# The RWKV stage of a two-block transformer kernel, reordered: gates, key norms, `widen`, mixing and exponentials in new places

## The chip, the cores and the metric

The kernel runs on one core of a Trainium2 chip. The metric is the device time of one execution in microseconds, as the median of several runs. All data is 32-bit floating point.

## What is computed

The reference is a chain of two transformer layers over one sequence of 256 tokens of width 1024. The first layer (two blocks deep, attention and MLP) is not touched. The second mixes tokens by a long convolution (Hyena) and by an RWKV-7 recurrence, weighs both by sigmoid gates, and then runs 16 experts of which each picks its 32 best tokens. What the change touches is this part of the reference:

```python
kk = heads(k * p['rw_k_k']).astype(jnp.float32)
kk = kk * lax.rsqrt(jnp.maximum(jnp.sum(kk * kk, axis=-1, keepdims=True), 1e-24))
k_mod = heads(k * (1.0 + (a - 1.0) * p['rw_k_a']))
...
def step(S, inp):                                   # in each direction, 8 heads of 64
    sa = jnp.einsum('bhij,bhj->bhi', S, a_t)
    S = S * w_t[:, :, None, :] + sa[..., None] * b_t[:, :, None, :] + v_t[..., None] * k_t[:, :, None, :]
    y = jnp.einsum('bhij,bhj->bhi', S, inp[5]) if emit else None
...
y_hy = hyena_branch(hy_cols, p) @ p['hy_proj']
y_rw, finals = rwkv_branch(rw_cols, p, states0)     # head norms, bonus, gate of its own at the end
g_hy, g_rw = jnp.split(jax.nn.sigmoid(gate_cols), 2, axis=-1)
mixed = (g_hy * y_hy + g_rw * (y_rw @ p['rw_proj'])) @ p['w_out']
```

A context of 256 tokens runs through the recurrence in both directions first, and its final states start the recurrence over the 256 tokens of the sequence.

## The kernel before

Weights come from HBM in chunks of 2 MB through SyncE's queue into a ring of four slots, later into more. A chunk is issued when the last job of the chunk that was in its slot is done on TensorE. Each product is a job with a PSUM bank of its own (eight banks in turn). The class `Jobs` writes down the order of jobs, which engine empties each bank, and which job is a chunk's last. `rwkv_steps()` writes down the order of steps in the RWKV stage, and TensorE, VectorE, ScalarE and GpSimd each walk through it and do their part. So the order of steps is the order in all four queues. Every engine works strictly in that order.

**The front.** The raw tiles (`rw` 4 to 11, eight products of 512 columns each over `w_in`) feed the mixing of neighbouring tokens (`mix`, VectorE, six instructions for two tiles) for the context (`ctx`) and the sequence (`lat`). Tiles 8 to 11 are the values. In between stand `lora` (two small products of 64 rows, `lw` and `la`, with sigmoids on ScalarE), `scan` and `centre` (sums of log decays on VectorE), `kraw`, `ksq`, `kk`, `kinv` (the key norm: square on ScalarE, mean over 64 rows on TensorE with a 128 x 128 matrix of 1/64, so that each value appears 64 times, square root on ScalarE, reciprocal and product on VectorE, all over 1024 columns), `exp` (exponentials of the decay sums on ScalarE), `km` and `mul` (the operands, on VectorE). `exp` waits for `kk_ready`.

**The groups.** There are four: g = 0 and 1 are the context forwards and backwards, 2 and 3 the sequence. Each solves a triangular system for its two chunks of 128 tokens: `NT` (scores), masks on GpSimd, `pick`, `spread` and a chain of small VectorE operations (blocks of eight, `blocks_solved`), `widen` (sixteen products with 32 contracted rows each, four for each of four tiles, then a masked copy by VectorE), `T` (transposes), `AK` (scores), then levels 3 to 5 with `W`, `XT` and `T` each, then `W6` and `XT6`. `W` is copied by VectorE; `XT`, `T` by ScalarE. The operands of group n = g + 1 are made inside group g.

**The state chain.** While group g begins, the state of group q = g - 1 is carried over its two chunks: `S0` (scale the state, VectorE), `U0`, `U`, `Y` (only for q of 2 and 3) and `S`, each waiting for the copy of the one before. The loop `for g in range(5)` has a fifth turn with only this chain, for q = 3. Behind it come bonus, group norm of the heads (`gmean`, `gvar`, with a reciprocal of 1024 columns), `gup`, then the eight `gates2` products (L1827), which need the chunks `gates2` 0 to 3, then `branch2`, `wo2`, norms, router and experts. The lines that matter:

```python
out.extend((("hold", 0, k), None, 0, 0, 0, 0, 0) for k in range(4))   # the ring as working space
cols("gates2", "w_in_2", 0, 3328, 5376)
...
elif what == "XT6":                     # releases hold 0, 1; ("S", 3, 1) releases hold 2, 3
    add((what, g, *at), "v", [("hold", 0, 0), ("hold", 0, 1)] if (g, *at) == (3, 1) else [])
```

`gates2` chunk k takes the slot of `hold` k. `product()` and `turn()` (L2529, L2541) are helpers, so most matmuls have one of these two lines. A matmul of 32-bit data appears in the trace as two records.

## Time and profile before

| what | value |
|---|---|
| median of three runs | 2928.76 us (2928.3 to 2930.73) |
| the profiled execution | 2929.43 us, span 2927.6 us |
| TensorE matmul busy | 2596.9 us (89%) |
| VectorE busy | 832.7 us (28%) |
| ScalarE busy | 539.1 us (18%) |
| GpSimd busy | 107.5 us (4%) |
| mean granted TensorE clock | 0.913 |
| from HBM | 663.98 MB, 227 GB/s over the span |

The profile is of one execution; the time of a run holds 1.8 us around the span. A granted clock of 1.00 is 2.4 GHz, 0.50 is 1.2 GHz. Busy shares are averages over stages with different limits, so stages are read by stretches of the timeline: up to some 1315 us the first layer, to 1471 us convolution and raw tiles, to 1841 us the RWKV groups and head norms, to 2052 us gates, output and router, then the experts.

### The profile page before, as it was taken

Reading aid. Unit: us, or ns where it says so; the run is one execution under the profiler, and the core shown is the slowest. Engines: PE = TensorE matmul, PEld = TensorE weight load, DVE = VectorE, ACT = ScalarE, POOL = GpSimd, SP = SyncE. Lnnn points to the kernel's source line nnn. Section 1 sums busy time; section 2 is a strip of 40 time slices with the busy share of each in tenths; the row PEclk is TensorE's granted clock in tenths of the full one; section 3 lists DMA queues with packets and bytes.
Section 4 is the critical chain, followed back from the end, with each engine's and each line's share of the span. In section 5 each row is a group of like instructions: output and inputs, shape, how many; then the busy total and the mean of one; then the engine's idle time right before and its main releaser. Section 6 shows DMA issues by size and latency. Waiting matters only on the chain.

```text
span 2927.6 us, 37135 instructions
## 1 busy us (share of the span) xinstructions
PE 2596.9 (89%) x15696; PEld 1840.4 (63%) x15696; DVE 832.7 (28%) x1479; ACT 539.1 (18%) x1068; POOL 107.5 (4%) x116
## 2 busy tenths in 40 slices
PE   6999999999999999999978899999778677777777
PEld 4757677887757778887568888775334333333333
DVE  2533421002634412002585542222111111111112
ACT  2115411001116211002233422111000000000001
POOL 0100000000100010000011110000000000000000
PEclk8999999999999999999988888998877887888788
DMA  7335755444332663342000001446999999999998
GB/s 303 118 117 226 315 204 201 148 166 182 137 130 87 244 256 134 129 152 103 0 1 1 1 2 58 172 195 254 428 429 429 428 429 427 429 429 428 429 428 359
DMA packets 48721, 666.72 MB, mean 228 GB/s; under 512 B 5498, under 2 KB 5669, under 8 KB 7520
## 3 DMA queue, kind: packets, MB, share of 16 engines
q1 hardware_dynamic: 46656, 656.65, 55.5%
q0 software_dynamic: 1952, 8.40, 0.8%
q8 instruction: 91, 1.49, 0.2%
q14 instruction: 22, 0.18, 0.0%
HBM read 663.98 MB, written 1.05 MB: 227 GB/s over the span
## 4 chain that ended last, share of the span: by engine, by line
PE 67%; DMA 25%; DVE 5%; ACT 2%; issue 1%; POOL 0%; DVEq 0%; POOLq 0%
PE bank L2529 53%; DMA ring<-exp_w 23%; PE bank L2537 7%; PE bank L2541 2%; PE bank L2739 2%; PE bank L1764 1%; DMA arena<-x 1%; PE bank L2558 1%; DMA arena<-exp_w 1%; PE bank L1790 1%; ACT hT L2090 0%; DVE hT L2411 0%; ACT arena L2214 0%; PE bank L2759 0%; DVE arena L1247 0%
## 5 line engine op out<-in xcount | busy, mean ns | idle before, releaser
L2529 PE MATMUL bank<-hT,ring 128*128 128x256 f32 (+2 forms) x3232 | 743.6, 391 | 9.6 <-ACT hT L2090 6.3
L2529 PEld LDWEIGHTS bank<-hT,ring 128*128 128x128 f32 x3232 | 615.0, 195 | 141.0 <-issue 60.8
L2537 PE MATMUL bank<-ring,arena 128*32 128x512 f32 (+1 forms) x2528 | 302.4, 615 | 134.3 <-DMA ring<-exp_w 132.5
L2529 PE MATMUL bank<-arena,ring 128*128 128x256 f32 x1600 | 349.5, 381 | 5.9 <-POOL arena L2062 2.7
L2529 PEld LDWEIGHTS bank<-arena,ring 128*128 128x128 f32 x1600 | 304.6, 191 | 49.0 <-POOL arena L2062 3.6
L2537 PEld LDWEIGHTS bank<-ring,arena 128*32 128x32 f32 x2528 | 83.3, 120 | 300.5 <-issue 191.5
L2537 PE MATMUL bank<-arena 128*32 128x256 f32 (+1 forms) x1552 | 180.2, 626 | 75.6 <-DMA arena<-exp_w 61.6
L2529 PEld LDWEIGHTS bank<-vec,arena 128*128 128x128 f32 x1344 | 181.3, 217 | 85.7 <-issue 78.7
L2529 PE MATMUL bank<-arena 64*128 64x128 f32 (+4 forms) x1156 | 208.1, 377 | 12.2 <-DVE arena L1340 11.3
L2529 PE MATMUL bank<-vec,arena 128*128 128x32 f32 (+2 forms) x1344 | 189.1, 294 | 4.9 <-ACT arena L2095 4.9
L2529 PEld LDWEIGHTS bank<-arena 64*128 64x128 f32 (+1 forms) x1156 | 140.5, 197 | 71.4 <-issue 60.0
L1533 DVE COPY arena<-bank 128x512 f32<-128x512 f32 x64 | 44.3, 692 | 482.6 <-PE bank L2537 482.6
L2537 PEld LDWEIGHTS bank<-arena 128*32 128x32 f32 x1552 | 61.0, 143 | 186.9 <-issue 113.2
L2368 DVE RECIPROCAL arena<-arena 128x512 f32<-128x512 f32 x28 | 93.9, 3353 | 118.4 <-ACT arena L2142 118.4
L2529 PE MATMUL bank<-ring 128*128 128x128 f32 (+1 forms) x1024 | 106.2, 263 | 1.3 <-DVE ring L1350 1.3
L2529 PEld LDWEIGHTS bank<-ring 128*128 128x128 f32 (+1 forms) x1024 | 103.5, 178 | 3.8 <-DVE ring L1350 1.5
L2529 PE MATMUL bank<-ring,hT 128*128 128x512 f32 (+1 forms) x256 | 97.5, 539 | 0.0
L1148 ACT ACTIVATE arena<-bank 128x512 f32<-128x512 f32 x64 | 38.2, 597 | 286.3 <-PE bank L2537 286.3
L2537 PE MATMUL bank<-ring,hT 128*32 128x512 f32 x576 | 70.4, 618 | 14.0 <-DMA ring<-ada_w 14.0
L2529 PEld LDWEIGHTS bank<-ring,hT 128*128 128x128 f32 x256 | 48.6, 190 | 48.4 <-issue 46.9
L1005 ACT ACTIVATE ring<-bank 128x512 f32<-128x512 f32 x112 | 60.9, 603 | 97.9 <-PE bank L2529 57.0
L2492 DVE TENSOR_TENSOR arena<-arena,bank 128x512 f32<-128x512 f32 x32 | 22.0, 688 | 197.7 <-ACT arena L2222 197.7
(306 smaller groups left out, 1974.5 us busy)
## 6 DMA issues: line engine op xcount, KB each, us to landing
ring<-exp_w SPq DMA_DIRECT2D x126, 2048.0 KB, 26.4
arena<-exp_w SPq DMA_DIRECT2D x65, 2048.0 KB, 25.7
ring<-w_in SPq DMA_DIRECT2D x38, 2048.0 KB, 8.2
ring<-ada_w SPq DMA_DIRECT2D x24, 2048.0 KB, 10.0
ring<-w_mlp_up SPq DMA_DIRECT2D x16, 2048.0 KB, 8.3
ring<-w_mlp_down SPq DMA_DIRECT2D x16, 2048.0 KB, 8.1
ring<-mod_w SPq DMA_DIRECT2D x12, 2048.0 KB, 8.3
ring<-w_out SPq DMA_DIRECT2D x6, 2048.0 KB, 8.1
```

The lines of the kernel that those rows point to most:

```text
L1005: free(sc.activation(out_, b, ACT.Identity), key)
L1148: done(sc.activation(raw_row(2 * q), b[:, :], ACT.Identity), ("up1", k0, q))
L1533: done(v.tensor_copy(raw_row(2 * q + 1), b[:, :]), ("up3", k0, q))
L1764: mms.append(nc.tensor.matmul(banks[par][:, p * 64:(p + 1) * 64], a, c, start=(i == 0), stop=(i == 1)))
L1790: mms.append(nc.tensor.matmul(banks[par][part, p * P:(p + 1) * P], a, c, start=(i == 0), stop=(i == 2)))
L2368: chain(v.reciprocal(rs, rs))
L2492: free(v.tensor_tensor(r, r, b[:, :], ALU.mult), ("up", l, i))
L2529: mm = nc.tensor.matmul(out_, a, b, start=(i == 0), stop=(i == len(pairs) - 1))
L2537: mm = nc.tensor.matmul(o, a, b, start=(i < 4), stop=(i >= len(pairs) - 4))
L2541: return nc.tensor.transpose(out_, in_, ident[0:in_.shape[0], 0:in_.shape[0]])
L2558: mm = nc.tensor.matmul(b[:, 0:SEQ], mean1024, sq[:, k], start=(k == 0), stop=(k == KT - 1))
L2739: mm = nc.tensor.matmul(banks[i][:, 0:SEQ], w[:, k, i * P:(i + 1) * P], ar(A_OA, 8, SEQ)[:, k], start=(k == 0), stop=(k == KT - 1))
```

## The change

It reorders the RWKV stage and alters four products in it:

- `gates2` 0 to 3 are steps of the last state chain, 4 stands behind `gmean`, 5 behind `gvar`, 6 and 7 behind `gup`, on TensorE and ScalarE. Their results move from arena column 0 to 10496, and the router's load moves behind the eight additions of `mix`, because it would land there.
- `kk` writes compact norms: four products with 32 output columns each, one below the other in one bank, so that root, `max` and reciprocal run over 256 columns. The new step `kwide` spreads the result over the heads with four products of 32 rows, and VectorE multiplies from the banks. The matrices for both (`C_HEADS`, `C_WIDE`) are loaded behind `solve` over constants that are no longer used.
- `widen` issues its sixteen products across the four row groups in turn, into four banks; `lora` issues `lw` and `la` in pairs.
- In the front, `mix ctx` 8 and 10 go behind `NT` and `widen` of group 0, `rw` 11 behind `mul`; `vt` 0 and `mix lat` 4 go to level 3 of group 0. In group 1, `kinv` goes behind the level-3 `T`, `kwide` ahead of and `exp` behind the level-4 `T`.
- `keep_busy` multiplies a constant into a bank that is written anew afterwards: two pairs of records ahead of `widen` in group 0 and ahead of `U0` of the second chunk, one ahead of its `U` (q below 3).

```diff
@@ rwkv_steps
     yield "rw", 8
+    yield "kk", 0
     yield "rw", 9
-    yield "kk", 0
+    yield "kinv", 0
+    yield "kwide", 0
     yield "rw", 10
-    yield "kinv", 0
     yield "exp", 0
-    yield "rw", 11
-    yield "mix", "ctx", 8
-    yield "mix", "ctx", 10
     yield "km", 0
     yield "mul", 0
-    for g in range(5):
+    yield "rw", 11
+    for g in range(4):
...
             if g == 0:
-                yield "vt", 0
-                yield "mix", "lat", 4
+                yield "mix", "ctx", 8
...
             for tile in range(4):
                 yield "widen", g, tile
+            if g == 0:
+                yield "mix", "ctx", 10
...
                 if lev == 3:
+                    yield "vt", 0
+                    yield "mix", "lat", 4
                     yield "mix", "lat", 6
                     yield "mix", "lat", 8
...
                     yield "vt", 1
-                    yield "kinv", 1
-                    yield "exp", n
...
+            if lev == 4 and n == 2:
+                yield "kwide", 1
             for tile in range(4):
                 yield "T", g, lev, tile
             if lev == 3 and n == 2:
                 yield "kk", 1
+                yield "kinv", 1
+            if lev == 4 and n == 2:
+                yield "exp", n
...
+    yield "S0", 3, 0
+    yield "BK", 3, 0
+    yield "U0", 3, 0
+    yield "BK", 3, 1
+    yield "U", 3, 0
+    yield "Y", 3, 0
+    yield "S", 3, 0
+    yield "S0", 3, 1
+    yield "gates2", 0
+    yield "U0", 3, 1
+    yield "gates2", 1
+    yield "U", 3, 1
+    yield "gates2", 2
+    yield "Y", 3, 1
+    yield "S", 3, 1
+    yield "gates2", 3
@@ Jobs
+    def gates2(self, i):
+        self.add(("gates2", i), "s", [("gates2", 0, i // 2)] if i % 2 else [])
@@ GpSimd
-            pool.dma_start(cst[:, C_SPREAD:], t["solve"]).then_inc(solve_loaded, 16)
+            pool.dma_start(cst[:, C_SPREAD:], t["solve"][:, 0:NCONST - C_SPREAD]).then_inc(solve_loaded, 16)
+            for at, n in ((C_HEADS, 0), (C_WIDE, 1)):
+                pool.dma_start(const(at), t["solve"][:, NCONST - C_SPREAD + P * n:NCONST - C_SPREAD + P * n + P]).then_inc(solve_loaded, 16)
...
-            pool.wait_ge(yrw_ready, 2)
-            pool.dma_start(ar(E_ROUTER, KT, N_EXP), t["router"].rearrange("(a p) n -> p a n", p=P)).then_inc(router_loaded, 16)
-            pool.dma_start(ar(E_SLOTS, CAP), t["slots"]).then_inc(router_loaded, 16)
             for j in range(8):
                 ...
+            pool.dma_start(ar(E_ROUTER, KT, N_EXP), t["router"].rearrange("(a p) n -> p a n", p=P)).then_inc(router_loaded, 16)
+            pool.dma_start(ar(E_SLOTS, CAP), t["slots"]).then_inc(router_loaded, 16)
@@ ScalarE
-                    for hf in range(2):
-                        b = filled(act, ("kk", g, hf))
-                        free(sc.activation(ar(R_ROOT + 512 * hf, 512), b[:, :], ACT.Sqrt, scale=64.0), ("kk", g, hf))
+                    b = filled(act, ("kk", g))
+                    free(sc.activation(ar(R_ROOT, SEQ), b[:, 0:SEQ], ACT.Sqrt), ("kk", g))
@@ VectorE
-                    emptied(dve, ("kk", g, 1))
-                    inv = ar(R_ROOT, 1024)
+                    emptied(dve, ("kk", g))
+                    inv = ar(R_ROOT, SEQ)
                     chain(v.tensor_scalar(inv, inv, 1e-12, None, ALU.max))
-                    chain(v.reciprocal(inv, inv))
-                    v.tensor_tensor(ar(R_KK, 1024), ar(R_KK, 1024), inv, ALU.mult).then_inc(kk_ready, 1)
-                    dve.wait_ge(kk_ready, g + 1)
+                    v.reciprocal(inv, inv).then_inc(kk_inverted, 1)
+                elif what == "kwide":
+                    for ct in range(CT):
+                        b = filled(dve, (what, g, ct))
+                        free(v.tensor_tensor(kk[:, ct], kk[:, ct], b[:, 0:SEQ], ALU.mult), (what, g, ct))
+                    emptied(dve, (what, g, CT - 1))
+                    dve.sem_inc(kk_ready, 1)
@@ TensorE
+                    for ct in range(CT):
+                        mm = product(b[32 * ct:32 * ct + 32, 0:SEQ], [(const(C_HEADS, 32), ar(R_SQ + SEQ * ct, SEQ))])
+                    finish(mm)
+                elif what == "kwide":
+                    pe.wait_ge(kk_inverted, g + 1)
+                    banks = [start((what, g, ct), ct) for ct in range(CT)]
+                    for ct in range(CT):
+                        part = slice(32 * ct, 32 * ct + 32)
+                        finish(product(banks[ct][:, 0:SEQ], [(cst[part, C_WIDE:C_WIDE + P], ar(R_ROOT, SEQ, parts=part))]))
...
+                    banks = [start((what, g, tile), tile) for tile in range(4)]
+                    if g == 0:
+                        keep_busy(banks[0], 2)
                     pe.wait_ge(blocks_solved, g + 1)
                     for p in range(CT):
-                        mm = product(b[:, p * P:(p + 1) * P], [(cst[part, C_WIDEN + P * p:C_WIDEN + P * (p + 1)], solved[part])])
-                    finish(mm)
+                        mms = []
+                        for tile in range(4):
+                            part = slice(32 * tile, 32 * tile + 32)
+                            mms.append(product(banks[tile][:, p * P:(p + 1) * P],
+                                               [(cst[part, C_WIDEN + P * p:C_WIDEN + P * (p + 1)], solved[part])]))
+                    for mm in mms:
+                        finish(mm)
...
+                    if g < 3 and at[0] == 1:
+                        keep_busy(banks[0], 2)          # U0
...
+                    if g < 3 and at[0] == 1:
+                        keep_busy(b, 1)                 # U
...
+            gates(4)                                    # behind gmean
...
+            gates(5)                                    # behind gvar
...
+            gates(6)                                    # behind gup
+            gates(7)
```

## Rows read from the trace of the kernel before

**Rows 1.** The page: GB/s in 40 slices; a DMA issue, KB, us to landing.

```profile
GB/s 303 118 117 226 315 204 201 148 166 182 137 130 87 244 256 134 129 152 103 0 1 1 1 2 58 172 195 254 428 429 429 428 429 427 429 429 428 429 428 359
...
ring<-w_in SPq DMA_DIRECT2D x38, 2048.0 KB, 8.2
```

**Rows 2.** SyncE's timeline of DMA issues: start us, us, what.

```profile
1794.37 35.43 SPq L2027 DMA_DIRECT2D ring<-w_in  x4
...
1924.38 0.80 SPq L2027 DMA_DIRECT2D arena<-exp_w  x2
```

**Rows 3.** Stretches: us, busy time of each engine, TensorE's clock, DMA share, GB/s.

```profile
1471.40:1808.00 336.60, 298.21 (x2812) 276.32 (x2812) 185.24 (x328) 115.60 (x220) 40.81 (x32) 0.86 0.04 14
1808.00:1841.30 33.30, 24.50 (x150) 17.57 (x149) 9.14 (x17) 6.67 (x9) 0.00 (x0) 0.74 0.32 126
```

**Rows 4.** TensorE's timeline, front and prices: start, us, line, op, [idle before <-releaser].

```profile
1425.27 2.96 PE L2529 MATMUL bank<-arena 64*128 64x256 f32 x16
1428.16 27.73 PE L2529 MATMUL bank<-hT,ring 128*128 128x512 f32 x64
...
1482.21 3.78 PE L2529 MATMUL bank<-arena 64*128 64x128 f32 x32 [10.86 <-DVE arena L1340]
...
1499.62 4.97 PE L2529 MATMUL bank<-rope,cst 32*128 32x128 f32 x32 [4.96 <-DVE rope L1368]
...
1671.44 2.06 PE L2529 MATMUL bank<-arena 64*128 64x128 f32 x32
...
1967.78 2.74 PE L1840 MATMUL bank<-cst 128*128 128x512 f32 x6
...
2041.74 1.93 PE L2537 MATMUL bank<-ring,arena 128*32 128x256 f32 x32
```

**Rows 5.** VectorE's timeline, front and prices.

```profile
1472.80 1.80 DVE L1247 SCALAR_TENSOR_TENSOR arena<-arena,vec 128x256 f32<-128x256 f32 x4
1474.76 1.38 DVE L1324 TENSOR_SCALAR arena<-arena,vec,stat 128x256 f32<-128x256 f32 x4 [0.16 <-DVE arena L1247]
...
1480.85 1.22 DVE L1340 SCALAR_TENSOR_TENSOR arena<-arena 128x1024 f32<-128x1024 f32 x1
...
1840.50 6.55 DVE L1425 RECIPROCAL arena<-arena 128x1024 f32<-128x1024 f32 x1 [4.00 <-ACT arena L1115]
...
1958.90 1.75 DVE L1457 RECIPROCAL arena<-arena 128x256 f32<-128x256 f32 x1 [0.93 <-ACT arena L1126]
```

**Rows 6.** TensorE's timeline, groups 1 and 2.

```profile
1563.02 0.63 PE L1764 MATMUL bank<-arena,ring 128*128 128x64 f32 x4 [1.93 <-DVE hT L1389]
...
1569.36 3.65 PE L2529 MATMUL bank<-hT,ring 128*128 128x64 f32 x16 [0.83 <-ACT hT L1005]
1572.94 5.13 PE L2529 MATMUL bank<-rope,cst 32*128 32x128 f32 x32
...
1589.77 3.81 PE L2529 MATMUL bank<-ring 128*128 128x128 f32 x32 [1.30 <-DVE ring L1350]
...
1614.83 3.65 PE L2541 MATMUL bank<-cst,ring 128*128 128x128 f32 x16 [9.76 <-ACT ring L1005]
...
1632.30 4.72 PE L2529 MATMUL bank<-arena 64*128 64x128 f32 x48 [0.47 <-DVE arena L1340]
```

**Rows 7.** Stretches of 2 us: us, TensorE busy, granted clock, DMA share, GB/s.

```profile
1552.00:1554.00 2.00, 2.00 (x11) 0.50 0.00 0
...
1576.00:1578.00 2.00, 2.00 (x15) 0.50 0.00 0
```

**Rows 8.** The chain of waits: start us, us, what (`U0` at either clock).

```profile
1563.02 5.55 PE bank L1764 x32
...
1795.75 3.87 PE bank L1764 x32
```

**Rows 9.** TensorE's timeline, the gates.

```profile
1841.31 55.42 PE L2529 MATMUL bank<-hT,ring 128*128 128x256 f32 x256
```

**Rows 10.** The DMA view: a GpSimd load, KB, us to landing.

```profile
arena<-x POOLq DMA_DIRECT2D x1, 1024.0 KB, 26.2
```

More of the change, by code:

```diff
@@ L81 @@
 NCONST = C_MASKB + 2 * 768
+C_HEADS, C_WIDE = C_MEAN128, C_ROT
 def shape_constants():
@@ L330, in rwkv_steps @@
             yield "S", q, 1
-        if not new:
-            return
         for tile in range(4):
@@ L518, in second_block @@
             elif what == "kk":
+                add(("kk", g), "s")
+            elif what == "kwide":
+                for ct in range(CT):
+                    add(("kwide", g, ct), "v")
+            elif what == "lora":
                 for hf in range(2):
-                    add(("kk", g, hf), "s")
-            elif what == "lora":
-                for half in ("lw", "la"):
-                    for hf in range(2):
+                    for half in ("lw", "la"):
                         add((half, g, hf), "s")
@@ L535, in second_block @@
                 self.raw(g)
+            elif what == "gates2":
+                self.gates2(g)
             elif what == "W" or what == "S":
@@ L544, in second_block @@
                 add((what, g, *at), "v")
-        for what, e in (("bonus", "v"), ("gmean", "v"), ("gvar", "s"), ("gup", "v")):
+        for what, e, *gates in (("bonus", "v"), ("gmean", "v", 4), ("gvar", "s", 5), ("gup", "v", 6, 7)):
             for hf in range(2):
                 add((what, hf), e)
-        for i in range(8):
-            add(("gates2", i), "s", [("gates2", 0, i // 2)] if i % 2 else [])
+            for i in gates:
+                self.gates2(i)
         for j in range(8):
@@ L1037, in second_scalar, with gates @@
             raw(3)
+            def gates(i):
+                b = filled(act, ("gates2", i))
+                free(sc.activation(ar(E_GATES + 512 * i, 512), b[:, :], ACT.Sigmoid), ("gates2", i))
             act.wait_ge(lora_mixed, 1)
@@ L1044, in second_scalar @@
                     raw(g)
+                elif what == "gates2":
+                    gates(g)
                 elif what == "ksq":
@@ L1115, in second_scalar @@
                 free(sc.activation(ar(R_ROOT + 512 * hf, 512), b[:, :], ACT.Sqrt, bias=col("rw_eps")), ("gvar", hf))
-            act.wait_ge(yrw_ready, 2)
-            for i in range(8):
-                b = filled(act, ("gates2", i))
-                free(sc.activation(ar(E_GATES + 512 * i, 512), b[:, :], ACT.Sigmoid), ("gates2", i))
+            for i in range(5, 8):
+                gates(i)
             sc.activation(stat[:, 62:63], eps, ACT.Sqrt)
@@ L1288, in second_vector @@
             for what, g, *at in rwkv_steps():
-                if what in ("rw", "mix"):
+                if what in ("rw", "mix", "gates2"):
                     s, d = None, None
                 else:
-                    s, d = group(2 * g) if what in ("kraw", "kinv") else group(g)
+                    s, d = group(2 * g) if what in ("kraw", "kinv", "kwide") else group(g)
                 if what == "kraw":
@@ L1629, in second_tensor, with keep_busy @@
                                              for m in range(4)]))
+            def keep_busy(b, n):
+                for _ in range(n):
+                    nc.tensor.matmul(b[:, :], ident, cst[:, 0:512], start=True, stop=True)
             pe.wait_ge(lora_loaded, 48)
@@ L1636, in paired, with gates @@
                 return [start((name, g, ci, par), par) for par in range(2)]
+            def gates(i):
+                w = chunk(("gates2", 0, i // 2))
+                columns(("gates2", i), w, (2 * (i % 2), 2 * (i % 2) + 1), lambda k: hT[:, 0, k], KT)
             for what, g, *at in rwkv_steps():
@@ L1640, in second_tensor @@
                     raw(g)
+                    continue
+                if what == "gates2":
+                    gates(g)
                     continue
@@ L1824, in second_tensor @@
                 finish(mm)
-            for i in range(8):
-                w = chunk(("gates2", 0, i // 2))
-                columns(("gates2", i), w, (2 * (i % 2), 2 * (i % 2) + 1), lambda k: hT[:, 0, k], KT)
+            gates(6)
+            gates(7)
             wh, wr = chunk(("hyp", 0, 0)), chunk(("rwp", 0, 0))
@@ L1835, in second_tensor @@
             work = ar(E_WORK, KT, SEQ)
-            def keep_busy(b, n):
-                for _ in range(n):
-                    nc.tensor.matmul(b[:, :], ident, cst[:, 0:512], start=True, stop=True)
             def mean_of(b, ready, i):
```

44 lines of the change are left out of this document (23 added, 21 removed).

## The prediction

> **What bounds the kernel now.** I read the page first. Its GB/s line shows two regimes [rows 1]: from about 2050 us to the end the DMA engines move some 428 GB/s, all they ever do, and between 1460 and 1790 us they move nothing worth naming. So the expert stage is bound by its weights, and the RWKV stage before it by something else. The question for any saving is then whether the expert weights start earlier with it. SyncE's timeline [rows 2] says yes: the first two expert chunks are issued at 1924.38, when the eighth `branch2` product is done, and the next ones at later steps of TensorE. Nothing in that queue starts by a time of its own. A microsecond that TensorE saves before 1924 us moves the whole stream, and I count it in full.
>
> Then I cut TensorE's busy time and clock into stretches [rows 3]. From the last raw tile to the last chain it is busy 298.2 of 336.6 us at a mean clock of 0.86; in the last chain and head norms (1808 to 1841.3) 24.5 of 33.3 us at 0.74. Both idle time and the half clock are there to win. TensorE's timeline and the chain of waits name the places, part by part.
>
> **1. The front: raw tiles, key norm, first operands.** TensorE idles 10.86 us ahead of the first `NT` at 1482.21, released by VectorE's last multiply [rows 4]. VectorE's queue shows why [rows 5]: a reciprocal of 1024 columns (6.55 us, as the one at 1840.50), a product, the mixing of `ctx` 8, then tile 11's copy, the mixing of `ctx` 10 (to 1474.6), then `km` and `mul`, 7.3 us (1474.76 to 1482.07). Now the reciprocal is over 256 columns (1.75 us, as the one at 1958.90) and both mixings come after `NT`. New order by rows: the paired `lora` (part 3) brings all 1.05 us forward. `kk` becomes 8 matmul records with 32 output columns; in [rows 4] 32 such records of 256 columns take 1.93 us, so 0.5 for 8. `kwide` I take at 0.8: bounds 0.5 (four at once) and 8 x 0.217 = 1.7. Raw 8, `kk`, raw 9, `kwide`, raw 10 then end at 1440.95 + 6.93 + 0.5 + 6.93 + 0.8 + 6.93 = 1463.0 (a raw tile is a quarter of the 27.73 us in [rows 4]; tile 7 ended at 1442.0). ScalarE copies tile 10 (0.7), loads its table (1.28) and makes two exponentials (2.1): 1467.2. `km` and `mul` add 7.3 and the issue 0.15: `NT` at 1474.8 against 1482.2. **Gain 7.4.** Raw 11 (to 1469.9) is hidden in this. 5 us of idle time stay.
>
> **2. The first group pays for it.** What was taken off the front isn't gone: `ctx` 8 takes the place of `lat` 4 behind `NT`, so `NT` to solved blocks stays 17.4 us; `ctx` 10 (2.5 us, of which 1.80 are the four instructions in [rows 5]) goes ahead of `scan`, and `lat` 4 joins `lat` 6 and 8 in level 3. Count from the start of `widen` (1499.62). VectorE before: `widen` copies to 5.6, scan and centre to 11.6, `AK` and `W` copies, so `XT` of level 3 at 15.0. Now: `widen` w, four copies 2.5, mixing 2.5, scan 3.4, centre 2.6, `AK` 2.4, first `W` 0.65, issue 0.2: w + 14.3 = 15.8 with w = 1.5. Three mixings (7.45) behind `W` put its level-4 copy at 25.5 and `XT` there at 25.6, not 24.0; the group ends at 40.0 instead of 38.3. **Loss 1.7** (3.2 at half clock). `vt`, 1.1 us of TensorE, lies in the time that TensorE now waits.
>
> **3. `widen` round the row groups, and fillers.** `widen` is 32 records, 4.97 to 5.13 us [rows 4, 6], all at half clock (0.50, [rows 7]). Pairs of 64 rows cost 2.06 us for 32 records at full and 3.78 at half clock [rows 4, 6]. I take w = 1.5 at full (bounds 0.9, four at once at the 0.114 us of a record with 128 rows, and 2.1, no better than pairs) and 3.0 at half. The Trainium skill (TensorEngine Tiling (Array Packing), Theoretical Speedup) allows up to 4 times for 32 rows: by it w is about 1.25, by the pairs 2.1. The same page (Key Properties) says that a change of the tiling mode drains the engine; no row here isolates such a drain.
> `lora` was 2.96 us for 16 records; as pairs I take 1.9 (bounds 1.5 and 2.96): 1.05 each, in groups 0 (counted), 1 and 2.
> What `widen` gives is cut by VectorE. In group 1, before, `widen` start to `XT` of level 3 is 16.8 us, and behind the first copy it is all VectorE: four copies, scan, `S`, centre, `kraw`, `AK`, `W` [rows 6]. Now w + 13.6: 15.1 (gain 1.7) or at half clock 16.6 (0.2). Group 2, without `kraw`: w + 12.5 against 17.4, gain 3.4 or 1.9. Group 3, no scan, TensorE bound: 5.1 - w = 3.6 or 2.1, and `Y` there 1.4 faster at full clock.
> Fillers: two matmul pairs ahead of `U0`, one ahead of `U`. A filler of 512 columns costs 0.91 us (2.74 for three, [rows 4]). They fill waits of 1.93, 1.92 and 1.23 us, and 0.83 us: so they cost 0.1 in groups 1 and 2 and 0.7 in group 3. If they hold the clock, `U0` goes from 5.55 to 3.87 and `U` from 3.65 to about half, 1.94 [rows 6, 8]: 3.4 in groups 1 and 2, and 2.0 in group 3, whose `U0` was slow only at its end. Sums, full or half clock: group 1 1.05 - 0.1 + 3.4 + 1.7 = 6.0 or 1.1; group 2 7.7 or 2.8; group 3 6.3 or 1.4. Does the clock hold? For: a `U0` with next to no idle time ahead (1795.75) runs at full speed. Against: at 1552 us the clock is 0.50 without idle time [rows 7]. I take the middle: 3.5 + 5.2 + 3.9 = **gain 12.6**.
>
> **4. The third exponentials.** In group 1 TensorE idles 9.76 us ahead of the level-4 `T` at 1614.83 [rows 6]. ScalarE stands in its queue at `exp`, which waits for VectorE's `max`, reciprocal (6.55) and product, 8.5 us, and the four `XT` copies stand behind it. Now: `kk` 0.5, table and root to 2.4 behind it, 256-column reciprocal; the first `W` copy of level 4 at 10.7 us after the level-3 `XT` start, so `XT` at 10.8 (one more 0.35 wait), `kwide` to 15.2, `T` to 17.0. `exp` then runs (4.6) under `W` of level 5 (3.7), and `T` ends at 26.2 instead of 38.0. With `W6` and `XT6` 30.2; but `km` and `mul` (9.0) start only when `exp` is done at 22.2, so the next `NT` is at 31.4, not 42.5 [rows 6]. **Gain 11.1**, and a wait of about 1.2 stays ahead of that `NT`.
>
> **5. Gates in the last chain and in the head norms.** All 55.3 us of `gates2` stand behind the norms [rows 9]. From the end of `S` 3,0 (1808.0) to the first `branch2` (1896.56) are 88.6 us. Moved between the links they cover the 8.8 us of idle time and the half clock that [rows 3] show there. At full rate: gates 55.3, `U0` 3.87, `U` 1.94, `Y` 3.9, `S` 1.1, bonus and means 3.7, variances 1.9, `gup` 1.8: 73.5. **Gain 15.1.** Checked: chunk 0 and 1 are issued from 1794.37 [rows 2]; the first lands 8.2 us later [rows 1], at 1802.6, the second one transfer (2 MB at 428 GB/s, 4.9 us) behind it: ahead of the first gate at 1808 and the third at 1819. Chunk 2 can load only once `S` 3,1 is done; the fourth gate (6.9) and bonus and means (3.7) leave it 10.6 us, where such a chunk lands in 8.2 [rows 1]. The tail of norms on VectorE, 12.1 us from its reciprocal (1840.50, [rows 5]) to the last product, starts 0.8 us after the variances; gates 5 to 7 and `gup` (22.5) cover it. ScalarE's extra table loads (1.28 each) lie there too.
>
> **6. The rest, at nothing.** Two more small constant loads stand in GpSimd's queue, which idles 3 us behind the old one. The router's load goes behind the additions of `mix`, into the expert stream; TensorE needs it 42 us later (from about 1926, just behind the first expert chunks in [rows 2], to the fillers at 1967.78 in [rows 4]), and the slowest landing of any GpSimd load is 26.2 us [rows 10].
>
> **Sum.** 7.4 - 1.7 + 12.6 + 11.1 + 15.1 = 44.5 us off the profiled execution's 2929.43: 2884.9; the median of the runs is 0.67 lower: **2884.3 us**. Everything at full clock gives 51.6 (2877), everything in part 3 at half clock 35.5 (2893).
>
> **Rivals.**
> *The clock falls as before* (15%): low-density groups are enough, fillers or not. Gain 32 to 37: 2892 to 2897. For it speaks 1552 us. The Trainium skill (TensorE: Matmul & The Clock Gate, A second HAM failure mode) tells of micro-idles between matmul groups that make the clock oscillate; by that rule this is the outcome.
> *The clock holds everywhere* (17%): 2872 to 2879; it would also lift the 1714 to 1725 stretch, which I left slow.
> *Interleaving gives no overlap* (8%): w = 5.1 and copies that begin only behind it. VectorE's chain starts later than before: 1.9 lost in group 1, like amounts elsewhere; with the full 7.4, 11.1 and 15.1 the gain is 22 to 30: 2899 to 2907.
> *The expert stream hides it* (2%): if the stream had its own start, no change, 2928. Against it: each issue in [rows 2] stands at a TensorE step.
> *Slower* (3%): the router's 1024 small pieces starve beside the expert chunks. Landing 85 us after issue or later (42 of slack plus the 44 saved) decides it; at 100 us it gives 2944. No row is near.
> Forecast, gain 38 to 50: 55%, 2879 to 2891.
>
> The range from 2872 to 2902 leaves out most of the last three and the far half of the no-overlap case. A difference of 0.2% (6 us) is about what this kernel's times can tell from none: faster 0.94, same 0.02, slower 0.04.
>
> **What would show it.** First `NT` near 1475; no wait of 9.8 us ahead of `T`; `widen` under 2 us a group with a clock of 1.00 in `U0` and `U`; no idle time over 1 us from 1800 to the first `branch2`; a stream of expert chunks that starts 44 us earlier. Wrong it would be by a new wait on a chunk of gates, by `W` copies stuck behind the mixings for longer than 2 us, or by a clock of 0.50 where I put 1.00.

## The result

The changed kernel takes 2879.23 us (median of three runs, 2879.03 to 2882.24) against 2928.76 (2928.3 to 2930.73): a ratio of 0.9833, 95% interval 0.9814 to 0.9852. The forecast was 2884.3, its range 2872 to 2902. 49.5 us are gained where 44.5 were forecast. The profiled execution took 2879.03 us with a span of 2876.5; its mean granted clock is 0.930 (0.913 before).

### The profile page after: what moved, and what is told of

It is laid out like the page before. It is cut to its first block, busy times and chain, and to the rows that moved or that the text cites. A ratio compares the mean times of both kernels' runs of the same rounds, so it can differ in the third digit from the quotient of the medians.

```text
span 2876.5 us, 37230 instructions
## 1 busy us (share of the span) xinstructions
PE 2563.0 (89%) x15742; PEld 1806.9 (63%) x15742; DVE 820.3 (29%) x1485; ACT 536.7 (19%) x1066; POOL 108.5 (4%) x118
## 4 chain that ended last, share of the span: by engine, by line
PE 66%; DMA 26%; DVE 5%; ACT 2%; issue 1%; POOL 0%; DVEq 0%; ACTq 0%; POOLq 0%
PE bank L2595 53%; DMA ring<-exp_w 25%; PE bank L2603 7%; PE bank L2607 2%; PE bank L2805 2%; PE bank L1832 1%; DMA arena<-x 1%; PE bank L2624 1%; PE bank L1860 1%; ACT hT L2156 0%; DVE hT L2477 0%; ACT arena L2280 0%; PE bank L2825 0%; DVE arena L1283 0%; DVE ring L1387 0%
## 5 line engine op out<-in xcount | busy, mean ns | idle before, releaser
L2595 PEld LDWEIGHTS bank<-hT,ring 128*128 128x128 f32 x3232 | 607.8, 192 | 139.2 <-issue 63.3
L1216 ACT ACTIVATE arena<-bank 128x128 f32<-128x128 f32 x64 | 17.7, 277 | 320.6 <-PE bank L2595 320.6
```

Of the source, the lines that this page charges most:

```text
L1216: sc.activation(ar(E_SL + 128 * q, 128), b[:, 0:128], ACT.Silu).then_inc(silu_ready, 1)
L2595: mm = nc.tensor.matmul(out_, a, b, start=(i == 0), stop=(i == len(pairs) - 1))
```

## The profile after

The page, GB/s in 40 slices, as in [rows 1]:

```profile
GB/s 310 119 107 230 305 236 205 147 146 205 117 124 111 191 256 173 143 146 114 30 1 2 1 2 59 176 235 314 428 428 429 429 428 429 428 429 428 429 428 356
```

SyncE's timeline, the chunks of gates and the first expert chunks, as in [rows 2]:

```profile
1757.22 45.76 SPq L2093 DMA_DIRECT2D ring<-w_in  x4
...
1871.41 0.80 SPq L2093 DMA_DIRECT2D arena<-exp_w  x2
```

The expert stream still runs at 428 GB/s and starts 53.0 us earlier (1924.38 before; 3.1 of it were there ahead of the first `lora`, where nothing was changed). So what the RWKV stage saved came through to the end, as the forecast had argued from the issue times.

Stretches of the changed kernel: front (first `lora` to first `NT`), groups 0, 1 and 2 (`NT` to the next `NT`), group 3 (to `U0` 3,0), last chain with norms and gates (to the first `branch2`). Columns as in [rows 3].

```profile
1422.20:1471.90 49.70, 44.98 (x129) 19.92 (x129) 22.45 (x43) 15.03 (x30) 0.00 (x0) 0.98 0.00 0
1471.90:1532.90 61.00, 52.91 (x490) 48.96 (x490) 52.13 (x98) 25.22 (x48) 10.59 (x8) 0.91 0.01 1
1532.90:1606.30 73.40, 68.97 (x688) 61.63 (x686) 42.42 (x82) 33.82 (x62) 10.07 (x8) 0.95 0.01 2
1606.30:1680.30 74.00, 71.83 (x726) 65.54 (x726) 44.52 (x83) 30.14 (x57) 10.14 (x8) 0.93 0.01 2
1680.30:1758.60 78.30, 76.10 (x813) 67.88 (x813) 33.45 (x64) 22.24 (x45) 10.07 (x8) 0.96 0.02 4
1758.60:1843.60 85.00, 84.22 (x541) 70.52 (x542) 20.95 (x26) 14.48 (x23) 0.00 (x0) 1.00 0.42 171
```

The same six stretches of the kernel before are 56.9, 59.7, 90.4, 76.6, 86.9 and 100.8 us long, at clocks of 0.94, 0.88, 0.83, 0.89, 0.86 and 0.92. TensorE's busy time fell from 424.1 to 399.0 us and its idle time from 47.2 to 22.4: of the 49.9 us saved, half is idle time. But 10.9 us of the busy time after are the new fillers (22 records of L1674), which do no work of the kernel. Without them TensorE works 388.1 us. So the 49.9 us are 24.8 of idle time and 36.0 of work done faster, less 10.9 for the fillers. TensorE ran at half clock for 109 us between 1300 and 1900 us before, and for 38 now. Read the last row across: in the sixth stretch TensorE is busy 84.22 of 85.00 us at 1.00.

TensorE's timeline, front, against [rows 4]:

```profile
1444.90 0.64 PE L2595 MATMUL bank<-arena,cst 128*32 128x256 f32 x8
...
1452.54 0.71 PE L2595 MATMUL bank<-arena,cst 32*128 32x256 f32 x8
...
1471.91 5.99 PE L2595 MATMUL bank<-arena 64*128 64x128 f32 x48 [4.73 <-DVE arena L1380]
...
1483.37 1.88 PE L1674 MATMUL bank<-cst 128*128 128x512 f32 x4
1489.22 1.24 PE L2595 MATMUL bank<-rope,cst 32*128 32x128 f32 x32 [3.96 <-DVE rope L1408]
```

`kk` and `kwide` take 0.6 to 0.7 us each, the wait ahead of `NT` has shrunk from 10.86 to 4.73, and `widen` takes 1.24 instead of 4.97.

VectorE in the front, against [rows 5]:

```profile
1447.72 1.75 DVE L1342 RECIPROCAL arena<-arena 128x256 f32<-128x256 f32 x1
...
1464.46 1.38 DVE L1364 TENSOR_SCALAR arena<-arena,vec,stat 128x256 f32<-128x256 f32 x4 [9.78 <-ACT stat L1121]
```

VectorE now waits 9.78 us for ScalarE's exponentials ahead of `km`; before, it had waited 0.16 there.

TensorE's timeline, group 1, against [rows 6]:

```profile
1553.40 0.63 PE L1832 MATMUL bank<-arena,ring 128*128 128x64 f32 x4 [0.20 <-DVE hT L1429]
...
1557.19 1.12 PE L1674 MATMUL bank<-cst 128*128 128x512 f32 x2
1558.16 1.91 PE L2595 MATMUL bank<-hT,ring 128*128 128x64 f32 x16
1560.00 1.17 PE L2595 MATMUL bank<-rope,cst 32*128 32x128 f32 x32
...
1567.50 1.16 PE L2595 MATMUL bank<-arena 64*128 64x128 f32 x16 [1.97 <-DVE hT L1445]
1568.59 5.47 PE L2595 MATMUL bank<-ring 128*128 128x128 f32 x32
1574.65 3.81 PE L2595 MATMUL bank<-ring 128*128 128x128 f32 x32 [0.59 <-DVE ring L1390]
...
1589.93 1.97 PE L2607 MATMUL bank<-cst,ring 128*128 128x128 f32 x16
...
1606.28 4.09 PE L2595 MATMUL bank<-arena 64*128 64x128 f32 x36 [1.45 <-DVE arena L1380]
```

Read it from the top. Fillers (L1674) stand where the waits of 1.93 and 0.83 us were, `U` takes 1.91 instead of 3.65, `widen` 1.17 instead of 5.13, `T` of level 4 (1589.93) has no wait of 9.76 us any more, and 1.45 are left ahead of the next `NT`. One line is new: 1.97 us of idle time inside `AK`, released by VectorE's emptying of the bank that `S` had filled (L1445), and behind it `W` at half clock, 5.47 where 3.84 is its full-clock time. The forecast had no such wait.

TensorE's timeline, the first three gates, against [rows 9]:

```profile
1770.80 7.17 PE L2595 MATMUL bank<-hT,ring 128*128 128x256 f32 x32
...
1781.53 15.87 PE L2595 MATMUL bank<-hT,ring 128*128 128x256 f32 x80
```

They fill the state chain (the 15.87 us are two gates and `U`) without a wait between them. No gate waits for its chunk: all of TensorE's idle time in the 85 us is 0.78 us, ahead of the first `Y`.

## The experiments

All times are medians of four or five runs. The kernel before took 2928.2 to 2929.7 us beside them.

**The changed kernel again.** It is told first, since it says how the others are to be read.

> The changed kernel once more, unaltered, to see how far the same code scatters from run to run. If the stretch from the first lora to the first branch2 (421.4 us in its first profile) repeats within 1 us, differences of 5 us between my one-part kernels are theirs. If it moves by 3 to 5 us, with stretches of half clock in other places, then differences of that size in single stretches (the tails of two experiments, 3 to 6 us longer at half clock) belong to the clock and not to the step that was moved.

Measured: 2877.99 us (2876.97 to 2889.51, five runs), ratio 0.9831 (0.9818 to 0.9844). The profiled run was the slowest, and its stretch from `lora` to `branch2` took 433.0 us instead of 421.4, with the same instructions. Its stretches of group 1 and of the last chain (73.4 and 85.0 above):

```profile
1535.80:1614.80 79.00, 73.28 (x688) 65.17 (x686) 42.45 (x82) 33.68 (x62) 10.08 (x8) 0.89 0.01 1
...
1768.70:1857.80 89.10, 88.32 (x540) 73.79 (x541) 20.96 (x26) 14.62 (x23) 0.00 (x0) 0.94 0.40 163
```

The clock is lower in both, 0.89 for 0.95 and 0.94 for 1.00. The stage came only 2.6 us later. Half clock takes 65 us of this profile and 38 of the first. In group 1 it covers `U` and `widen`, though the fillers stand ahead of them:

```profile
1564.11 3.52 PE L2595 MATMUL bank<-hT,ring 128*128 128x64 f32 x16
1567.55 2.09 PE L2595 MATMUL bank<-rope,cst 32*128 32x128 f32 x32
```

So stretches of half clock move from execution to execution and made a difference of 11.6 us in the stage here; the kernel before scatters by 3.7 us in nine runs beside it. A difference of 4 or 5 us in a single stretch is therefore only a part's own where the clock there is the same or where a wait shows it. Pooled, the changed kernel's eight runs have a median of 2879.1 us; I compare with that.

**Gates behind `gup` again.**

```diff
-    yield "gates2", 0        # and 1, 2, 3, between the links
...
-            gates(4)         # gmean
...
-            gates(5)         # gvar
...
+            for i in range(8):
+                gates(i)     # behind gup
```

> The changed kernel with all eight gate products behind the last product of the head norms again. If they cover waits and the half clock there (my theory), it is 15 us slower than the changed kernel (2879.2), so about 2894, and the stretch from the end of the third-last state product to the first product of the two branches takes about 88 us again, not 73. If the gain of the tail came only from idle time and the clock would rise anyway, 9 us: 2888. If the expert stream had hidden it, no difference.

Measured: 2896.11 us (2893.4 to 2903.17), ratio 0.9896 (0.9879 to 0.9912), 17.0 more than the changed kernel. `U0` 3,0 to `branch2` took 100.85 us instead of 84.99. TensorE's timeline shows the old waits:

```profile
1795.80 3.67 PE L2588 MATMUL bank<-arena,cst 128*128 128x512 f32 x8 [3.15 <-DVE arena L1446]
...
1801.49 1.95 PE L2588 MATMUL bank<-arena,cst 128*128 128x512 f32 x4 [2.02 <-ACT arena L1145]
...
1805.01 55.42 PE L2588 MATMUL bank<-hT,ring 128*128 128x256 f32 x256
```

15.9 us for this part: theory held. In this profile, too, the half clock is back for 17 us (1774 to 1791), as before the change.

**No fillers.**

```diff
-                    if g == 0:
-                        keep_busy(banks[0], 2)
...
-                    if g < 3 and at[0] == 1:
-                        keep_busy(banks[0], 2)
...
-                    if g < 3 and at[0] == 1:
-                        keep_busy(b, 1)
```

> The changed kernel without its three new places of filler matmuls; everything else stays. If they hold TensorE's clock in the state chain and at widen (theory), the clock falls to 0.50 in U0, U and widen of groups 1 to 3 and the kernel is 9 to 12 us slower (2888 to 2891), with widen at 2 to 3 us a group instead of 1.2. If the clock would hold without them, because widen and the pairs are short now, it is as fast as the changed kernel or up to 1 us faster.

Measured: 2894.54 us (2893.04 to 2897.36), ratio 0.9881 (0.9865 to 0.9898), 15.4 more. TensorE's timeline of its group 1, `U0`, `U` and `widen`:

```profile
1556.43 0.78 PE L1828 MATMUL bank<-arena,ring 128*128 128x64 f32 x4 [1.93 <-DVE hT L1429]
...
1563.67 3.64 PE L2589 MATMUL bank<-hT,ring 128*128 128x64 f32 x16 [0.83 <-ACT hT L1037]
1567.24 2.09 PE L2589 MATMUL bank<-rope,cst 32*128 32x128 f32 x32
```

The waits of before are back to the hundredth (1.93, 0.83). `U` takes 3.64 and `widen` 2.09, at half clock, here in all three groups; the second profile of the changed kernel has about the same in groups 1 and 2 (3.52 and 2.09) with fillers, and the full clock in group 3 alone. So these rows do not show by themselves what the fillers do. In the profiled executions TensorE ran at half clock for 85 us between 1300 and 1900 us, against 38 in the changed kernel's first profile and 65 in its second. Stretch for stretch against the second, which began at the same time, it lost 6.0 us, against the first 17.6. The median says 15.4, more than the 9 to 12 expected, and the slowest of the changed kernel's eight runs (2889.51) is faster than the fastest here (2893.04). So the fillers earn time, some 15 us by the medians; how much of it in one execution depends on where the half clock falls. They cost little: from the product ahead of them to `U0` TensorE takes 1.92 us in group 1 as before, and in group 3 1.55 for 1.23.

**`widen` one tile after the other.**

```diff
+                    tile = at[0]
+                    part = slice(32 * tile, 32 * tile + 32)
+                    b = start((what, g, tile))
                     for p in range(CT):
-                        for tile in range(4):
-                            mms.append(product(banks[tile][...], [(cst[part, ...], solved[part])]))
+                        mm = product(b[...], [(cst[part, ...], solved[part])])
+                    finish(mm)
```

> The changed kernel with the sixteen products of widen tile by tile again. Theory: the row groups overlap only when they alternate, so widen takes at full clock 2.5 to 3.7 us instead of 1.2, and as VectorE's first copy starts behind a quarter of it, each group loses 0.5 to 2 us: 2 to 6 us in all, 2881 to 2885. Rival: the gain at widen was the clock alone, then widen takes about 2.5 us and nothing is lost that VectorE does not hide: below 1.5 us.

Measured: 2888.68 us (2882.31 to 2895.08), ratio 0.9866 (0.9846 to 0.9886), 9.6 more. TensorE's timeline, `widen` of groups 0 and 1:

```profile
1492.23 5.13 PE L2590 MATMUL bank<-rope,cst 32*128 32x128 f32 x32 [4.31 <-DVE rope L1408]
...
1565.16 2.82 PE L2590 MATMUL bank<-rope,cst 32*128 32x128 f32 x32
```

This splits the term. In the old order the sixteen products cost 2.82 us at full clock (groups 1 to 3) and 5.13 at half; in the new order 1.17. Of the 3.7 to 4.0 us by which the change made `widen` shorter in groups 0 and 1, some 1.65 are the row groups and 2.2 to 2.3 the clock. 2 to 6 us were expected for the whole kernel: a miss in size. The stage was 5.5 us longer than in the first profile of the changed kernel and 6.1 shorter than in the second, and the runs scatter by 12.8 us, so no more than the rows of `widen` themselves can be taken from this run.

**Third exponentials back ahead of the level-4 `T`.**

```diff
                 if lev == 4:
                     yield "vt", 1
+                    yield "kinv", 1
+                    yield "kwide", 1
+                    yield "exp", n
...
-            if lev == 4 and n == 2:
-                yield "exp", n
```

(`kinv` and `kwide` are taken out of their new places too.)

> The changed kernel with kinv, kwide and the third exponentials ahead of the level-4 XT again, the norms still compact. If the order made the gain (theory), TensorE idles again at that place: kwide waits 3 us for the reciprocal and T some 5 us for ScalarE, 7 to 9 us slower than the changed kernel, 2886 to 2888. If the short reciprocal alone made it, under 3 us slower.

Measured: 2883.14 us (2879.47 to 2888.97), ratio 0.9851 (0.9834 to 0.9867), 4.0 more. TensorE's timeline, `kwide` and the level-4 `T`:

```profile
1587.89 0.71 PE L2593 MATMUL bank<-arena,cst 32*128 32x256 f32 x8 [1.90 <-DVE arena L1340]
...
1595.12 2.09 PE L2605 MATMUL bank<-cst,ring 128*128 128x128 f32 x16 [2.75 <-ACT ring L1035]
```

Two waits, 4.65 us, stand where before one of 9.76 stood; `widen` to `W6` of group 1 is 4.8 longer and 1.0 comes back as the wait ahead of `NT`. 7 to 9 were expected, and under 3 by the other theory: a miss in size, between the two. The place alone is worth 3.8 us once the norms are compact.

**Norms over 1024 columns, in the new places.**

```diff
-                    for ct in range(CT):
-                        mm = product(b[32 * ct:32 * ct + 32, 0:SEQ], [(const(C_HEADS, 32), ...)])
-                    finish(mm)
+                    for hf in range(2):
+                        b = start(("kk", g, hf))
+                        finish(product(b[:, :], [(mean64, ar(R_SQ + 512 * hf, 512))]))
```

> The changed kernel with the key norms over 1024 columns again (two products with the mean matrix, a reciprocal of 6.55 us), in the new places. Theory: in the front nothing changes by more than 0.5 us, because the reciprocal ends at about 1459, ahead of the copy of tile 10 that ScalarE waits for; in group 1 the level-4 copies of W wait for it and TensorE idles 6 to 8 us: 2886 to 2888. Rival: the compact norms also set the first NT, then it is 3 us or more later too and the kernel is over 2889.

Measured: 2886.07 us (2882.51 to 2887.74), ratio 0.9848 (0.9833 to 0.9863), 6.9 more. `lora` to `NT` took 49.91 us, `widen` to `W6` of group 1 49.14 instead of 40.81. VectorE's timeline there:

```profile
1586.17 6.55 DVE L1338 RECIPROCAL arena<-arena 128x1024 f32<-128x1024 f32 x1
```

and TensorE's, the level-4 `XT`:

```profile
1594.86 5.59 PE L2580 MATMUL bank<-ring 128*128 128x128 f32 x32 [6.52 <-DVE ring L1382]
```

The expectation was right in time. Compact norms earn 8.3 us from `widen` to `W6` in group 1, because there the reciprocal stands ahead of the `W` copies: 6.5 are this wait and 1.8 the half clock on `XT` behind it (5.59 for 3.81). They earn 0.2 in the front, where VectorE waits for ScalarE anyway.

**The front's old order.**

```diff
     yield "exp", 0
+    yield "rw", 11
+    yield "mix", "ctx", 8
+    yield "mix", "ctx", 10
     yield "km", 0
     yield "mul", 0
-    yield "rw", 11
```

(`vt` 0 and `lat` 4 go back too.)

> The changed kernel with raw tile 11 and both context mixings ahead of km and mul, and vt and the mixing of lat 4 behind NT, as in the kernel before; the norms stay compact. Theory: the first NT is 5 to 6 us later, group 0 gives 1.4 us back, so 4 us slower, 2883. Rival: the compact norms made the gain in the front, then this is within 1 us of the changed kernel.

Measured: 2883.6 us (2878.32 to 2885.57), ratio 0.9838 (0.9823 to 0.9853), 4.5 more. TensorE's timeline, first `NT`:

```profile
1481.60 2.72 PE L2594 MATMUL bank<-arena 64*128 64x128 f32 x22 [10.86 <-DVE arena L1379]
```

10.86 us, the wait of [rows 4] to the hundredth, although the norms are compact here. `lora` to `NT` is 6.1 us longer, `widen` to `W6` of group 0 3.1 shorter: 3.1 net, where 4 were expected. Elsewhere in this profile the last chain is 5.7 us longer at a clock of 0.92, which this edit does not touch and of which the changed kernel's second profile shows 4.2 as well, and groups 1 and 3 are 3.1 shorter.

**`scan` behind `S`,** to remove the new wait inside `AK`.

```diff
-            if ahead:
+            if ahead and g == 0:
                 yield "scan", n
         if old:
...
             yield "S", q, 1
+        if ahead and g > 0:
+            yield "scan", n
```

> The changed kernel with VectorE's scan behind the copies of S in groups 1 and 2. The wait of 1.97 us in the middle of AK goes (AK's last bank is that of S, which VectorE empties behind scan). Theory: group 2 gains 2.4 us, its wait and the half clock of its W (5.46 instead of 3.8 us); group 1 gains nothing at XT, as VectorE's queue ends at the same time; in all 2 to 3 us, 2876 to 2877. Rival: both groups stay bound by VectorE, no difference.

Measured: 2887.72 us (2884.25 to 2890.15), ratio 0.9859 (0.9843 to 0.9874), 8.6 more: a miss, on the wrong side. TensorE's timeline, `AK`, `W` and `XT` of group 1:

```profile
1564.71 2.06 PE L2597 MATMUL bank<-arena 64*128 64x128 f32 x32
1566.70 3.84 PE L2597 MATMUL bank<-ring 128*128 128x128 f32 x32
1574.99 5.93 PE L2597 MATMUL bank<-ring 128*128 128x128 f32 x32 [4.45 <-DVE ring L1392]
```

`AK` has no wait, `W` is at full clock; but VectorE's sum is what it was, so all of it stands as one wait of 4.45 us ahead of `XT`, which starts 14.66 us behind `widen` for 14.65 in the changed kernel and then runs at half clock. That half clock is the 2.1 us by which `widen` to `W6` is longer. In group 2 it is 1.0 shorter, where 2.4 were expected. How much of the 8.6 belongs to that and how much to where the half clock fell is open: see the next pair.

**A front of its own, and with `scan` behind `S`.** The front's mixings go into the time in which VectorE waits there.

```diff
     yield "kk", 0
+    yield "mix", "lat", 4
     yield "rw", 9
     yield "kinv", 0
     yield "kwide", 0
+    yield "exp", 0
+    yield "mix", "ctx", 8
     yield "rw", 10
-    yield "exp", 0
     yield "km", 0
     yield "mul", 0
+    yield "mix", "lat", 6
     yield "rw", 11
```

(The three mixings are taken out of their places in group 0.)

> The kernel before with a better order than the change: scan behind S, and the front with the mixing of lat 4 ahead of kinv, ctx 8 behind exp and lat 6 behind mul, exp ahead of raw tile 10, no mixing between NT and the solved blocks, only lat 8 in level 3. By VectorE's idle times in the changed kernel's front (4.9, 3.8 and 9.8 us) the first NT can start at 1467.2, when raw tile 11 is done, 4.7 us earlier; the solved blocks come 1 to 2.6 us sooner behind it; level 4 of group 0 loses its wait of 0.6; with the 2.4 us of group 2 about 9 us: 2869 to 2872. Rival: what is taken from the front is waited for at the next place, under 4 us.

> The front alone of the last version: mix lat 4 ahead of raw 9 and of kinv, exp ahead of raw 10, ctx 8 behind it, lat 6 behind mul; scan stays ahead of S. Theory 1 (the front gives 7.5 us, 4.8 to NT and 2.7 to the solved blocks, and the scan's move was a loss of 2 in group 1 against 2 gained in the next one): the stretch from lora to branch2 takes 412 to 415 us, as in the version with both (413.1), some 2869 to 2873 us. Theory 2 (the scan's move cost 8 us by itself, as it did alone, whatever the front): 5 us or more faster than the version with both, 2864 or less.

Measured: with both edits 2868.93 us (2867.92 to 2881.15), ratio 0.9803 (0.9787 to 0.982); the front alone 2872.84 (2868.6 to 2873.56), 0.9807 (0.9794 to 0.982). TensorE's timeline of the front alone, the last raw tiles and the first `NT`:

```profile
1456.03 14.00 PE L2594 MATMUL bank<-hT,ring 128*128 128x512 f32 x32
1469.96 3.78 PE L2594 MATMUL bank<-arena 64*128 64x128 f32 x48
```

No wait is left ahead of `NT`: 44.94 us for 49.73, and 14.64 for 17.31 from there to `widen`, in both kernels. 7.5 us are gained, as worked out for the second of the two (the first had 4.7 and 1 to 2.6). The stage takes 413.5 us with the front alone and 413.1 with both: theory 1 held. So here `scan` behind `S` was worth nothing that shows (0.4 us less in the stage, 3.9 less in the medians, with ranges that overlap), where on the changed kernel it had cost 8.6: that edit has no effect of its own that these runs settle.

**Fillers inside `AK`.**

```diff
+                    if (what, *at) == ("AK", 1) and g in (1, 2):
+                        b = start((what, g, 1, 0))
+                        keep_busy(b, 2)
                     banks = paired(what, g, at[0])
```

> The changed kernel with two fillers (1.8 us) between the two banks of the second AK, groups 1 and 2, where TensorE waits 1.97 us for the bank that S left. Theory (idle time among small matmuls drops the clock): the fillers stand in time that was idle, W behind them runs at full clock, 3.84 instead of 5.46 us, in both groups: 3.2 us less in the stretch, and the two dips at 1606 and 1616 may go as well, another 2 to 3: 421.4 becomes 415 to 418.5. Rival (W's half clock has another cause, such as its 64-column records): W stays at 5.4, and the stretch is the same or 0.3 us longer.

> Both of the above. If they are independent, the gains add: 7.5 us from the front and 3 to 5 from the fillers, 410 to 412 us for the stretch, about 2866 to 2869 us in all, the fastest of all kernels. If the clock's phase decides (where an episode of half clock falls), the sum can be off by 3 to 5 us to either side.

Measured: alone 2883.14 us (2878.95 to 2890.83), ratio 0.9842 (0.9829 to 0.9856): inconclusive, 4.0 above the changed kernel with ranges that overlap. 415 to 418.5 us were expected for the stage; it took 432.8. The changed kernel's second profile began at the same time, took 433.0 and had `W` at full clock without these fillers, so this pair cannot tell. With the new front it is 2867.91 (2866.78 to 2869.82), ratio 0.9793 (0.9779 to 0.9806), the fastest of all by its median, with a range that overlaps that of the new front with `scan` behind `S` (from 2867.92). 410 to 412 us were expected for the stage. That pair can be laid side by side, since both began within 0.3 us. TensorE's timeline of group 1 with the front alone:

```profile
1562.57 1.28 PE L2594 MATMUL bank<-arena 64*128 64x128 f32 x16 [1.97 <-DVE hT L1444]
1563.78 5.31 PE L2594 MATMUL bank<-ring 128*128 128x128 f32 x32
1569.72 3.81 PE L2594 MATMUL bank<-ring 128*128 128x128 f32 x32 [0.63 <-DVE ring L1389]
```

and with front and fillers:

```profile
1561.65 0.59 PE L1673 MATMUL bank<-cst 128*128 128x512 f32 x1
1562.29 1.16 PE L2597 MATMUL bank<-arena 64*128 64x128 f32 x16
1563.38 3.84 PE L2597 MATMUL bank<-ring 128*128 128x128 f32 x32
1569.43 5.44 PE L2597 MATMUL bank<-ring 128*128 128x128 f32 x32 [2.21 <-DVE ring L1389]
```

In this pair the fillers do hold the clock: `W` takes 3.84 instead of 5.31. But `XT` starts at the same time to 0.3 us, because VectorE's copy of `W` releases it; the time went into the wait (2.21 for 0.63), and now `XT` is at half clock. Group 1 is 1.6 longer from `widen` to `W6`, group 2, where TensorE sets the pace, 1.6 shorter (40.05 for 41.67), and the stage is the same (413.9 for 413.5): the gains do not add. The 4.9 us between the medians lie elsewhere: in the profiles, 3.2 of them behind `branch2`, which neither edit touches.

## Why the prediction came out right

Gains by stage, forecast and measured in the two profiles of the changed kernel against the one of before:

| stage | forecast | first profile | second profile |
|---|---|---|---|
| front, `lora` to `NT` | 7.4 | 7.2 | 7.2 |
| group 0 | -1.7 | -1.3 | -1.6 |
| group 1 (3.5 + 11.1) | 14.6 | 17.0 | 11.4 |
| group 2 | 5.2 | 2.6 | 2.4 |
| group 3 | 3.9 | 8.6 | 7.2 |
| last chain, norms, gates | 15.1 | 15.8 | 11.7 |
| sum | 44.5 | 49.9 | 38.3 |

In the first profile another 3.1 us come ahead of `lora` and 1.9 are lost behind `branch2`, both outside the change: 51.1 us of span. The median gained 49.5. The forecast of 44.5 lies between the stages of the two profiles, 49.9 and 38.3. That is what a middle value gives and no proof of it: part 3 measured 17.3 us in one and 10.1 in the other for 12.6.

**Part 1** was right to 0.2 us, the wait of 5 us that should stay measured 4.73. The reason was right only in half: the forecast named the short reciprocal and the mixings together. The old order with compact norms has the old wait of 10.86 us, the new order with wide norms loses 0.2. Of the two it was the mixings, with `rw` 11 (6.1 us); the rest is the paired `lora` (1.0). The part's own terms end at 1474.7, not at 1474.8.

**Part 2** was right: a loss of 1.4 to 1.7 us from `widen` to `W6` for 1.7. The run with the front's old order takes it apart: 38.33 us before, 36.70 there, 39.76 in the changed kernel. The mixings cost 3.1, and the rest of the change gave 1.6 back.

**Part 3**, 12.6 us forecast, is the term that was mis-sized. `widen` took 1.17 us where 1.5 was taken, `lora` 2.00 where 1.9. The Trainium skill (TensorEngine Tiling (Array Packing), Theoretical Speedup) allows up to 4 times for 32 rows, which gave an estimate of 1.25 from a row at half clock. At one and the same clock the runs show 2.82 against 1.17, 2.4 times: within its limit, and not near it. The wrong step is the middle between full and half clock: 3.5, 5.2 and 3.9 us for groups 1 to 3, where 6.1, 2.6 and 8.6 were measured in the first profile and 0.5, 2.4 and 7.2 in the second. The first profile has group 1 at the full-clock figure (`NT` to `XT` of level 3: 6.1 for 6.0), group 3 above it: 8.6 for 6.3. There `widen` and `Y` gave 5.4 us for the 5.0 taken, and the slow stretch at 1714 us that I had left as it was came back shorter (6.8 us of half clock, 1688 to 1695, for 10.2); in the second profile it lasted 10.2 again, and group 3 gave 7.2. Group 2 lies below the middle: 2.6 for 5.2. There two things fail against the 7.7 of the full clock: the clock falls behind the wait ahead of `NT` (half clock at 1606 to 1610 and 1616 to 1620; 3.2 us), and the faster TensorE meets VectorE earlier, inside `AK`, 1.96 us, with `W` at half clock behind it (2.0 us). The forecast counted VectorE's chain up to `XT`, and forgot that its next link, emptying the bank of `S`, also frees a bank for `AK`.

**Part 4** was right: from `XT` of level 3 to the next `NT` 42.53 us became 31.63, 10.9 for 11.1, with a wait of 1.45 for 1.2 ahead of that `NT`. Taken back alone, the place costs 3.8 and the compact norms 8.3, of which 1.8 are half clock. They are not the terms of a sum: together they make 12.1, more than the 10.9.

**Part 5** was right: 15.8 for 15.1 in the first profile, 8.8 of it idle time and 7.0 work done faster; no gate waited for a chunk, and taking this part alone back cost 15.9. The second profile gives 11.7, since half clock falls into its chain for 10.2 us.

**Part 6**, at nothing: the router's load, in the middle of the expert stream, landed 7.1 us after its issue (2.9 before), and the router's product began 74.8 us behind the first `branch2` as before. 1.9 us were lost behind `branch2` in the first profile, but 1.1 gained in the second.

**The rivals.** No overlap is excluded: the copies began behind 1.17 us. The clock that holds everywhere would have given 51.6 us (51.9 by the prediction's own terms, and 35.7 for the half clock, not 35.5); the median's 49.5 is nearer to that than to the forecast, yet 38 to 65 us of half clock are still there, so it did not hold. The clock that falls as before is excluded for the median and by the half clock itself (109 us before), and its mechanism is not: the second profile, at 2889.51 us, is close to that rival's 2892, and shows the prediction's own sign of being wrong, half clock in `U` and `widen` of groups 1 and 2. The Trainium skill (TensorE: Matmul & The Clock Gate, A second HAM failure mode) tells of small idle times that make the clock oscillate; the fillers' removal, 15.4 us, agrees with it, and so did the pair with and without fillers in `AK`. Why the clock fell in `U0` of group 1 in the second profile, behind the same wait of 0.20 us as in the first, no run shows.

## What to carry to other kernels

Where two engines take turns, first ask whose work the wait is. The gates are work of TensorE that waits for nobody, and between the links of a chain they took back 8.8 us of idle time and 7.0 us of slow work, while `scan` moved past `S` only put VectorE's time in group 1 from one wait into a longer one. Short constant matmuls in waits of 1 or 2 us cost almost nothing and gave 15.4 us in the medians, though they did not keep TensorE's clock up in every execution. They pay only if TensorE and not the other engine starts the next step. Once stretches of half clock matter, profile the same code twice before a stretch is read to the microsecond.

## What the runs showed of the hardware

- The same code, begun 2.6 us later, took 11.6 us longer in a stage of 421 us, by stretches at 1.2 GHz in other places; its runs scatter by 12.5 us, those of the kernel before by 3.7.
- In one execution, the one with norms over 1024 columns, the same wait of 1.96 us inside `AK` was followed by `W` at full clock in group 1 (3.84) and at half clock in group 2 (5.44). A single wait does not decide it, so what does stays open.

```profile
1569.46 1.16 PE L2580 MATMUL bank<-arena 64*128 64x128 f32 x16 [1.96 <-DVE hT L1437]
1570.55 3.84 PE L2580 MATMUL bank<-ring 128*128 128x128 f32 x32
...
1652.15 1.16 PE L2580 MATMUL bank<-arena 64*128 64x128 f32 x16 [1.96 <-DVE hT L1437]
1653.25 5.44 PE L2580 MATMUL bank<-ring 128*128 128x128 f32 x32
```

- Sixteen 32-bit products with 32 contracted rows cost 2.82 us tile by tile and 1.17 when they go round the four row groups, each with a bank of its own in both orders and both at full clock; sixteen 64-row records of `lora` 2.96 one by one and 2.00 in pairs.
